# All twelve input slices as split products, the first quad's down rows loaded by quarters, and two output pieces taken token half by token half

## The reference, cut to what matters

```python
def second_block(x, ...):
    for l in range(2):
        h = rms_norm_2(x, norm_mix_pre[l])
        proj = h @ w_in[l]                     # 1024 x 3072: twelve slices of 256 columns
        (c_a, c_gate, sb_q, sb_k, sb_v, r_q, r_k, r_v, r_g, sc_b, sc_c, sc_h) = jnp.split(proj, 12, axis=-1)
        y_conf = conformer_conv(c_a, c_gate, ...)      # 31 taps, layer norm, silu
        y_sb = merge_heads(stick_breaking_attention(...sb_q, sb_k, sb_v...))
        y_ret = retention_mixer(r_q, r_k, r_v, r_g, ...)
        y_sc = short_gated_conv(sc_b, sc_c, sc_h, ...) # 3 taps
        mix = jnp.concatenate([y_conf, y_sb, y_ret, y_sc], axis=-1) @ w_out[l]
        x = x + rms_norm_2(mix, norm_mix_post[l])
        f = conv_ffn(rms_norm_2(x, norm_ffn_pre[l]), ffn_up[l], ffn_conv_w[l], ffn_down[l])
        x = x + rms_norm_2(f, norm_ffn_post[l])
```

## Time and profile before

| | |
|---|---|
| median of 3 runs | 1450.93 us (1448.68 to 1452.49) |
| the profiled execution's own time | 1450.56 us |
| its span | 1448.7 us |
| matmuls, busy share | 85% (1224.7 us, 9311 instructions) |
| VectorE, ScalarE busy | 49%, 32% |
| transfers | 349.66 MB, mean 241 GB/s, 427 GB/s in slices 11 to 20 of 40 |

### The profile page before, as it was taken

One profiled execution on the slowest core, in us unless ns is written; L12 is line 12 of the kernel. 1 busy time (PEld: TensorE's weight loads), 2 busy tenths in 40 slices (PEclk: granted clock), 3 DMA queues, 4 the chain that ended last, 5 costly groups with the idle time before them and its releaser, 6 DMA issues.

```text
span 1448.7 us, 22087 instructions
## 1 busy us (share of the span) xinstructions
PE 1224.7 (85%) x9311; PEld 963.3 (66%) x9311; DVE 714.0 (49%) x1131; ACT 466.6 (32%) x668; POOL 2.9 (0%) x12
## 2 busy tenths in 40 slices
PE   6999999999464655636667999999999999999998
PEld 6988798795121212212222897799998897799997
DVE  4474754374010101101101579787776479777776
ACT  3542433232000000000001354654454354654543
POOL 0000000000000000000000000000000000000000
PEclk8999999999677878878778999999999999999999
DMA  8841301696999999999999553566654354566650
GB/s 257 281 147 34 88 4 30 231 358 274 428 427 427 426 426 428 428 427 427 427 426 394 187 180 105 159 191 194 184 174 146 131 175 117 146 205 187 191 159 30
DMA packets 178679, 349.66 MB, mean 241 GB/s; under 512 B 7884, under 2 KB 154481, under 8 KB 166546
## 3 DMA queue, kind: packets, MB, share of 16 engines
q1 hardware_dynamic: 178090, 347.59, 66.1%
q10 hardware_dynamic: 488, 0.62, 0.2%
HBM read 347.13 MB, written 3.43 MB: 242 GB/s over the span
## 4 chain that ended last, share of the span: by engine, by line
PE 51%; DMA 16%; DVE 7%; DVEq 3%; issue 2%; ACT 1%; SPq 1%; ACTq 0%
PE ps L2521 17%; DMA expert_ring<-in_w_expert_up 14%; PE ps L2559 11%; PE ps L1765 5%; PE ps L2507 5%; PE ps L1792 4%; PE ps L1806 2%; PE ps L1472 2%; PE ps L1753 2%; DVE att_T L2832 1%; DMA expert_ring<-in_w_expert_down 1%; DVE w_lo L2821 1%; DVEq L2833 1%; PE ps L2472 1%; SPq L1672 1%
## 5 line engine op out<-in xcount | busy, mean ns | idle before, releaser
L1765 PE MATMUL ps<-expert_ring,w_slot 128*32 128x512 f32 x768 | 144.1, 721 | 75.6 <-DMA expert_ring<-in_w_expert_gate 45.6
L1834 DVE TENSOR_TENSOR hT<-ps,hT 128x512 f32<-128x512 f32 x8 | 8.5, 1066 | 359.5 <-PE ps L1765 359.5
L2821 DVE TENSOR_TENSOR w_lo<-expert_early,w_hi 128x2048 fp32r<-128x2048 f32 x72 | 164.8, 2292 | 29.2 <-ACT w_hi L2653 28.0
L2653 ACT ACTIVATE w_hi<-expert_early 128x2048 fp32r<-128x2048 f32 x72 | 137.8, 1914 | 58.0 <-PE ps L2559 39.2
L1765 PE MATMUL ps<-expert_early,w_slot 128*32 128x512 f32 x256 | 73.7, 741 | 80.5 <-DMA expert_ring<-in_w_expert_up 42.8
L2521 PE MATMUL ps<-x_hi,w_hi 128*128 128x256 f32 x864 | 123.3, 283 | 0.0
L2521 PE MATMUL ps<-x_hi,w_lo 128*128 128x256 f32 x864 | 120.7, 282 | 0.0
L2521 PE MATMUL ps<-x_lo,w_hi 128*128 128x256 f32 x864 | 120.2, 280 | 0.5 <-DVE x_lo L2959 0.5
L1765 PEld LDWEIGHTS ps<-expert_ring,w_slot 128*32 128x32 f32 x768 | 36.1, 129 | 125.8 <-issue 125.8
L2521 PEld LDWEIGHTS ps<-x_hi,w_hi 128*128 128x128 f32 x864 | 111.4, 189 | 5.5 <-ACT x_hi L2761 1.8
L2521 PEld LDWEIGHTS ps<-x_hi,w_lo 128*128 128x128 f32 x864 | 110.6, 190 | 0.0
(11 more groups left out here) (477 smaller groups left out, 2048.0 us busy)
## 6 DMA issues: line engine op xcount, KB each, us to landing
expert_ring<-in_w_expert_gate SPq DMA_DIRECT2D x24, 2048.0 KB, 24.0
expert_ring<-in_w_expert_up SPq DMA_DIRECT2D x24, 2048.0 KB, 25.0
expert_ring<-in_w_expert_down SPq DMA_DIRECT2D x20, 2048.0 KB, 23.4
expert_early<-in_ffn_up SPq DMA_DIRECT2D x36, 1024.0 KB, 6.1
w_slot<-in_w_in SPq DMA_DIRECT2D x28, 1024.0 KB, 5.5
expert_early<-in_w_in SPq DMA_DIRECT2D x20, 1024.0 KB, 6.2
expert_early<-in_ffn_down SPq DMA_DIRECT2D x18, 1024.0 KB, 4.9
expert_early<-in_w_expert_gate SPq DMA_DIRECT2D x8, 2048.0 KB, 15.0
```

The source lines that it names most:

```text
L1765: mm = pe.matmul(m.ps[rows_of(e), b, :], x_quad[:, k, rows_of(e)], w[e][:, k, :], start=(k == 0), stop=(k == KC - 1))
L2653: act.activation(w_hi[:, i % SPLIT, :], raw_slot(m, i), ACT.Copy).then_inc(S["w_hi"], 1)
L2821: dve.tensor_tensor(w_lo[:, i % SPLIT, :], raw_slot(m, i), w_hi[:, i % SPLIT, :].bitcast(F32), ALU.subtract).then_inc(S["w_lo"], 1)
```

## The change

All twelve slices go through `product` or `values_product`; `WHOLE`, `whole` and `x32` are gone, conf_a moves to PSUM bank 3, and a half's slot is counted across layers (`half_slot`). The normed state is rounded out of PSUM straight into `x_hi`, and VectorE makes `x_lo` out of PSUM as it did in the feed-forward part. The order of splits, taps and score steps on ScalarE and VectorE is new. The scores are biased before `Abs`, so the separate masking multiplication is dropped. The pieces 0 and 1 of the second layer are split at the end of the first layer's feed-forward part. The third and fourth output pieces are taken for t = 0 both, then for t = 1 both. The split of piece 17 moves behind the second norm. In the expert stage the down rows of quad 0 are loaded by quarters f, each after two steps k of the gate product. SP reads the count of overflow blocks earlier. Fourteen spent semaphores of the recurrence are cleared for reuse.

```diff
@@ moe_part: expand, down, sync
+                if n == 0 and b == GATE and k % 2 and k < KC - 1:
+                    mm.then_inc(gate_quarters_used, 1)
...
             for f in range(FC):
+                if n == 0:
+                    pe.wait_ge(first_rows[f], 16 * 4)
...
-                for g in range(SLOTS_R, last_down):
+                for f in range(FC):
+                    if f < FC - 1:
+                        sp.wait_ge(gate_quarters_used, f + 1)
+                    else:
+                        sp.wait_ge(filled[GATE], 1)
+                    for g in range(SLOTS_R, SLOTS_R + 4):
+                        src = a["w_expert_down"][0, g - SLOTS_R].rearrange("(p c) n -> p c n", p=P)
+                        sp.dma_start(expert_chunk(m, "down", g % SLOTS_R)[:, f, :], src[:, f, :]
+                                     ).then_inc(first_rows[f], 16)
+                for g in range(SLOTS_R + 4, last_down):
                     await_used(sp, *divmod(g - SLOTS_R, len(CHUNKS)))
                     load_expert_chunk(sp, m, a, g)
+                over = over_blocks(sp)
@@ layers: sync, tensor
+    def half_slot(l, i):
+        return (l * PIECES + i) % SPLIT
...
-                if i - RAW < WHOLE:
-                    await_used(sp, l, i - RAW)
-                else:
-                    await_split(sp, l, "w_lo", i - RAW)
+                await_split(sp, l, "w_lo", i - RAW)
                 load_piece(sp, m, a, l, i)
...
-                if i < WHOLE:
-                    whole(i)
-                elif name in ("sb_v", "ret_v"):
+                if name in ("sb_v", "ret_v"):
                     values_product(free(name), i)
                 else:
-                    product(free(name), i, lambda k, j: k * 256 + j * P, h_ready(0) if i == WHOLE else None)
+                    product(free(name), i, lambda k, j: k * 256 + j * P, h_ready(0) if i == 0 else None)
...
-            for r, chunk in enumerate(OUT_ROWS):
-                signalled(pe, l, "y_split", r + 1)
-                mm = tokens_product(PIECE_OUT + r, banks, (x_hi, x_lo), chunk, r == 0, r == 3)
-                if r < 3:
+            for r, t in ((0, None), (1, None), (2, 0), (3, 0), (2, 1), (3, 1)):
+                tiles = range(TT) if t is None else (t,)
+                if t != 1:
+                    signalled(pe, l, "y_split", r + 1)
+                mm = tokens_product(PIECE_OUT + r, banks, (x_hi, x_lo), OUT_ROWS[r], r == 0, r == 3, tiles)
+                if r < 3 and t != 0:
                     mm.then_inc(S["out_used"], 1)
@@ layers: scalar
             root_of_state(0)
+            if l == 0:
+                split_piece(0)
             signalled(act, l, "vec_set", 1)
...
-                act.activation(x32[:, c, :], m.ps[:, b, c % 2 * SEQ:(c % 2 + 1) * SEQ], ACT.Copy,
-                               scale=v("norm_mix_pre_2", c)).then_inc(S["x32"], 1)
-                if c % 2:
-                    act.drain().then_inc(drained[b], 1)
-            for c in range(KC):
-                act.activation(x_hi[:, c, :], x32[:, c, :], ACT.Copy).then_inc(S["h_hi"], 1)
+                act.activation(x_hi[:, c, :], m.ps[:, b, c % 2 * SEQ:(c % 2 + 1) * SEQ], ACT.Copy,
+                               scale=v("norm_mix_pre_2", c)).then_inc(S["h_hi"], 1)
+            if l == 0:
+                split_piece(1)
+            split_piece(2)
+            split_piece(3)
             copy(s_["conf_gate"], "conf_gate", ACT.Sigmoid)
+            split_piece(4)
+            copy(s_["sb_q"], "sb_q", scale=HEAD ** -0.5)
             split_piece(5)
...
+                if q == len(FFN_ORDER) - 2:
+                    load_roots()
+                if q < len(FFN_ORDER) - 1:
+                    split_piece(PIECE_FFN + q + SPLIT)
@@ layers: vector
+            split_low(0 if l == 0 else 1)
             for c in range(KC):
-                signalled(dve, l, "h_hi", c + 1)
-                dve.tensor_tensor(x_lo[:, c, :], x32[:, c, :], x_hi[:, c, :].bitcast(F32), ALU.subtract
-                                  ).then_inc(S["h_lo"], 1)
+                if c % 2 == 0:
+                    signalled(dve, l, "h_hi", c + 2)
+                b = UNIT["turn_mix", c // 2][0]
+                dve.scalar_tensor_tensor(x_lo[:, c, :], m.ps[:, b, c % 2 * SEQ:(c % 2 + 1) * SEQ],
+                                         v("norm_mix_pre_2", c), x_hi[:, c, :].bitcast(F32),
+                                         ALU.mult, ALU.subtract).then_inc(S["h_lo"], 1)
+                if c % 2:
+                    dve.drain().then_inc(drained[b], 1)
+            if l == 0:
+                split_low(1)
+            split_low(2)
+            split_low(3)
...
+                b = await_filled(dve, l, "sb_score", h)
+                dve.tensor_tensor(sb_z[:, h, :], m.ps[:, b, 0:W3], m.c("past_neg"), ALU.add).then_inc(drained[b], 1)
+                dve.drain().then_inc(S["sb_biased"], 1)
...
-                dve.scalar_tensor_tensor(sb_l[:, h, :], m.ps[:, b, 0:W3], 0.0, sb_l[:, h, :], ALU.max, ALU.add
-                                         ).then_inc(drained[b], 1)
-                dve.drain()
-                dve.tensor_tensor(sb_l[:, h, :], sb_l[:, h, :], m.c("past"), ALU.mult).then_inc(S["sb_masked"], 1)
+                dve.scalar_tensor_tensor(sb_l[:, h, :], sb_z[:, h, :], 0.0, sb_l[:, h, :], ALU.max, ALU.add
+                                         ).then_inc(S["sb_masked"], 1)
```

More of the change, by code:

```diff
@@ L1732, in moe_part @@
         OVER_SLOTS = SLOTS_R - EARLY
+        gate_quarters_used = sem("gate_quarters_used")
+        first_rows = [sem(f"first_rows{f}") for f in range(FC)]
         over_landed = [sem(f"over_landed{k}") for k in range(OVER_SLOTS)]
@@ L2216, in _units @@
         use(("turn_mix", n), turns[n])
-    n = 0
-    for name, count in (("conf_a", 1), ("conf_gate", 1), ("sb_q", 1), ("sb_k", 1), ("vec", 1), ("ret_q", 1),
+    use(("conf_a", 0), 3)
+    n = 1
+    for name, count in (("conf_gate", 1), ("sb_q", 1), ("sb_k", 1), ("vec", 1), ("ret_q", 1),
                         ("sb_score", 4), ("ret_k", 1), ("ret_v", 1), ("swap", 2), ("tail", 4), ("sb_v", 1),
@@ L2495, in outputs @@
                     mm.then_inc(filled[b], 1)
-            def whole(i):
-                b = free(SLICES[i])
-                await_landed(pe, l, i)
-                raw = raw_slot(m, i)
-                for j in range(2):
-                    for k in range(KC):
-                        if i == 0 and j == 0:
-                            signalled(pe, l, "x32", k + 1)
-                        col = k * 256 + j * P
-                        mm = pe.matmul(m.ps[:, b, j * SEQ:(j + 1) * SEQ], raw[:, col:col + P], x32[:, k, :],
-                                       start=(k == 0), stop=(k == KC - 1))
-                mm.then_inc(filled[b], 1)
             def product(b, i, at, sync=None):
-                s = i % SPLIT
+                s = half_slot(l, i)
                 for j in range(2):
@@ L2542, in project, with tokens_product @@
                 i = SLICES.index(name)
[L2543 to L2545 removed]
+                if name in ("sb_v", "ret_v"):
                     values_product(free(name), i)
                 else:
[L2548 to L2553 removed]
+                    product(free(name), i, lambda k, j: k * 256 + j * P, h_ready(0) if i == 0 else None)
+            def tokens_product(i, banks, x, chunk, first, last, tiles=range(TT)):
+                s = half_slot(l, i)
+                for t in tiles:
                     for part, (xs, w) in enumerate(((x[0], w_hi), (x[1], w_hi), (x[0], w_lo))):
@@ L2950, in layers_vector @@
             split_y(0)
-            for i in range(15, PIECE_FFN + 2):
-                split_low(i)
+            split_low(15)
+            split_low(PIECE_FFN)
             post_norm("out", 2, 1)
```

99 lines of the change are left out of this document (53 added, 46 removed).

## The result

The changed kernel takes 1433.56 us, the median of four runs (1433.08 to 1433.85), beside 1449.81 for the kernel before in the same comparison (1446.20 to 1452.49). The ratio is 0.9889, with a 95% interval of 0.9866 to 0.9912: 16.2 us faster, inside the range, where 22.4 had been forecast. The profiled execution took 1433.79 us, its span is 1432.0 (before 1448.7). One execution of a later kernel (q_contig, the one that was profiled) took 3016 us and is left out of what follows.

A forecast was written before the change was run, and what follows sets the result against it. Bounds: transfers in the expert stage, TensorE in the layers. Gains of 4.5 (quarters), 9.6 (second mixer) and 8.2 us (first mixer) sum to 22.3 off 1450.56, giving 1428.5 us after adjusting to the median; range 1424 to 1437.

The forecast's parts named there:

- the quarters bring nothing: Rival, expert stage: quarters delay the up chunks or small transfers stay slow, losing the 4.5 us; 1433 us, chance 0.13.
- signs named for being wrong: TensorE waiting for `w_lo` among the slices, granted clock under 1 there, or 512 KB transfers under 380 GB/s.
- Quarters, 4.5 forecast: Expert stage, quad 0's down rows: earlier issue by quarters fills a transfer gap; 4.5 us gain, bounds 2 and 5.6.
- the whole gap goes: Expert stage, 345 to 356 us: early quarters recover all 5.55 us of transfer time lost at 212 instead of 428 GB/s.
- price of 1.05 us for the small transfers: Expert stage: 8.39 MB in 512 KB transfers at 406 instead of 428 GB/s cost 1.05 us.
- the whole stage moves by it: Expert stage: bound by transfers up to the last quad, so all of it shifts by the quarters' 4.5 us.
- Mixers, 8.2 and 9.6 forecast: First and second mixer: split slices, reordered VectorE work and earlier output pieces save 8.2 and 9.6 us.
- The wait there was forecast: First output piece's high-low part: TensorE waits at full clock for `w_lo` of piece 12, made after `split_y(6)` and centring.
- The tail, 0.5 forecast: End of each mixer: taking t = 0 first frees its banks 2.8 us earlier; gain 0.5 us, between 0 and 1.1.
- VectorE holds up the mixers: Rival, both mixers: VectorE has little slack, handovers cost 3.5 us per mixer; 1435.5 us, chance 0.17.
- the slower case: Rival, mixer slices: waits for late `w_lo` halve the clock, products take 11.3 instead of 5.66 us; 1496 us, chance 0.04.

The follow-up runs named there:

- q_contig: Changed kernel with each quarter of quad 0's down weights one contiguous 512 KB piece, so weights are permuted; 1432.93 to 1438.62 us, ratio 0.9910.
- q_late: Changed kernel with all quarters of the first down rows issued only after the whole gate product; 1438.34 us, ratio 0.9927.
- after: The changed kernel itself, with the whole change, against the kernel before; 1433.56 us, ratio 0.9889.
- q_only: Kernel before with only the first down rows by quarters and the semaphores they need cleared; 1448.23 us, ratio 0.9989 (0.9975 to 1.0004).
- q_halves: Changed kernel with the first quad's down rows in two halves of 1 MB instead of four quarters of 512 KB; 1431.19 us, ratio 0.9891.
- mix_only: Changed kernel with the first quad's down rows loaded as whole chunks behind the gate, as before; 1437.25 us, ratio 0.9915.
- low12: Changed kernel with VectorE's low half of piece 12 made ahead of the centring instead of behind it; 1431.21 us, ratio 0.9877.
- whole_tokens: Changed kernel with its last two output pieces taken whole again, not by token halves; 1434.10 us, ratio 0.9892.
- parts_first: Changed kernel with piece 12's low half early, first down rows in 1 MB halves, and first products after norms ordered by parts; 1426.58 us, ratio 0.9830.
- lows_back: Changed kernel with the second FFN weight piece split ahead of the norm again on ScalarE and VectorE, token halves kept; 1443.12 us, ratio 0.9944.

## Why the prediction was right, and where it was off

Against the kernel before, by the profiles: the first slice of mixer 1 comes 1.36 us sooner (801.48 to 800.12), mixer 1 is 7.17 shorter, mixer 2 7.81, the other parts together 0.36. The sum is 16.7, the difference of the spans. The terms had 4.5, 8.2 and 9.6, and each came out smaller. That the time still lies inside the range is owed to the room that the range gave to the rivals. That it equals the 1433 of the rival "the quarters bring nothing" is chance: half of what is missing, 2.8 us, is missing in the mixers. And one of the signs named for being wrong was there: the first 512 KB transfers ran under 380 GB/s.

**Quarters, 4.5 forecast, 1.4 measured.** Right: when the first is issued, and that its early issue is worth most of the gap (4.6 of 5.55 us, by q_late against after). The step that failed is "the whole gap goes", together with its price of 1.05 us for the small transfers. I had read 406 GB/s from the last down rows, in the middle of a full flow; at the head of one, quarters are at 168 to 291. From 345 to 356 us the mean of 317 GB/s leaves 11 x (1 - 317/428) = 2.9 us of the gap's 5.55. The price there is 2.3 us and not 1.05, and the gate of quad 1 comes 2.6 us sooner after the gather. The Trainium skill's page "DMA: Bandwidth & Descriptors" (section "Bandwidth") wants 1 MiB per transfer. I had set this rule aside with the 406; at the head of a flow the traces agree with it, in the fourth us transfers of 1 MB were at 451 GB/s, and those of 512 KB in after at 287, though they do not tell the size from the length of the rows.

The second part of the miss is "the whole stage moves by it". The last quad's up product comes 2.2 us sooner after the gather, the first slice only 1.2: the last down rows were just in time before, and are 1.35 us late now. Of the kernels in the table all but before, q_only and q_halves show this wait (0.43 to 2.38 us), mix_only too with 0.89 and no quarters at all. So the quarters alone are not its cause. All kernels with the wait have SP's earlier read of the overflow count, which before and q_only have not, but q_halves has it and no wait. What decides it was not settled. The 1.4 us are also one profile: by the time from gather to first slice, the five kernels with the same expert stage are between 2.6 us sooner than before and level with it.

**Mixers, 8.2 and 9.6 forecast, 7.2 and 7.8 measured.** The mechanism held: no wait for `w_lo` among the slices, VectorE's 9.85 us wait gone, the full clock between the slices and the norm, TensorE's last slice as the end. In mixer 2 the miss of 1.8 us has two places:
- The slices end 84.9 us after their start and not 84.0. The first product's high-low part begins after 4.65 us, not 4.01. I took that number from the second norm, where VectorE is free when `x_hi` is there; here it is still at the low half of piece 1 until 1117.60, and `x_lo` starts 0.47 us behind the first slice instead of 0.18 ahead of it. The same lines for piece 0 I had counted in mixer 1 (5.4, measured 5.43), not here.
- From the slices' end to the high-low part of the first output piece it is 5.16 us, not 4.4: 1.64 to the first output piece where I had 1.2, and VectorE's centring waits 0.53 for its bank.

The wait there was forecast, as the price of an order that I took as given. low12 shows that it was not: moving one instruction ahead of the centring takes 1.5 to 1.7 us out of each mixer.

**The tail, 0.5 forecast, 0.56 measured in mixer 2 (8.65 to 8.09), for the wrong reason.** I gave it to the token halves. whole_tokens shows that it belongs to the moved split alone. Before, VectorE's low half of the moved piece stood ahead of its update, and the update began when it was done (VectorE in the kernel before, second mixer):

```profile
1241.16 2.29 DVE L2821 TENSOR_TENSOR w_lo<-expert_early,w_hi 128x2048 fp32r<-128x2048 f32 x1 [2.35 <-ACT w_hi L2653]
...
1243.37 1.28 DVE L2801 TENSOR_TENSOR hT<-ps,post_gain 128x512 f32<-128x512 f32 x2
```

ScalarE's squares were not held up: they began at 1241.72, after a wait for TensorE. In whole_tokens, with the low half gone, VectorE's update of the first half ends 1.0 us after TensorE's last output product instead of 1.5; the update of the second half ends 3.8 us after it, in after as well, instead of 4.4. I had put the moved split at nothing, and did not ask when its slot is free: with token halves it had to move.

**The rivals.** "VectorE holds up the mixers" came true in part, for some half of its 3.5 us: the 1.8 us that mixer 2 falls short are mostly places where TensorE waits for VectorE, at the first `x_lo`, at `split_y(6)` and at the `w_lo` of piece 12. But it is not short of time, as that rival had it: it still has 3.85 and 2.04 us of idle time ahead of the pad in mixer 2, and low12 takes out 1.5 us by an order alone. "The quarters bring nothing" was closer than its 0.13 for this term: with an interval over no change, q_only can't tell it from zero, and only the stages can. The pauses among the slices, on which the slower case rested, did not come in after, and its slices ran at full clock.

## What to carry to other kernels

The rate of small transfers in the middle of a full flow says nothing of their rate at its head: there, give the size that comes up fastest (1 MB here) and issue it early. When a price is copied from a similar place, look at what the engine does just before, in both places. When work is moved off a norm, ask when the slot that it writes becomes free: an order that empties banks sooner can keep weights in use longer.

## What the runs showed of the hardware

The same instructions in the same order ran at two clocks. In the first product of a mixer, TensorE has pauses of 0.24 us for `x_lo`, two in the first mixer and one in the second (parts_first has one and none). In the eleven profiles with split first slices, the granted clock fell behind them to 0.50 (1.2 GHz) in five first mixers and one second mixer, and stayed at 1.00 (2.4 GHz) in the rest; it came back after about 3.4 us, in one case after more than 6. Window and timeline of TensorE in q_halves, first mixer:

```profile
799.00:802.00 3.00, 3.00 (x15) 2.98 (x15) 2.90 (x2) 0.44 (x1) 0.00 (x0) 0.50 1.05 380
```
```profile
798.63 0.97 PE L2528 MATMUL ps<-x_lo,w_hi 128*128 128x256 f32 x2 [0.24 <-DVE x_lo L2865]
799.40 1.91 PE L2528 MATMUL ps<-x_hi,w_lo 128*128 128x256 f32 x8
```

Eight matmuls take 1.91 us, and 1.11 in after at the same place of the second mixer. It costs 1.2 to 1.7 us a mixer (the star of the table; 2.4 in the long case), as much as the edits that were compared. That the pauses are its cause is not shown: the mixers that kept their clock have the same ones. parts_first has fewer of them and kept its clock in both mixers, but so did others; one profile of it does not show that it always will. The 1.41 us wait at the output piece never brought the clock down, where three waits within 6 us had the earlier trace rows, and so had the one of 3.39 us in lows_back.

The Trainium skill's page "TensorE: Matmul & The Clock Gate" (section "A second HAM failure mode: psum-queue depth-cycling") tells of frequent short pauses between groups of matmuls that throw the clock back and forth. The traces agree in so far as the clock fell where the longest pause in the product was 0.24 us; here it fell once in a mixer, and in 6 of 22 mixers. That it happens in some executions and not in others is from these runs.
